# One block's MLP and the next block's differential attention joined in one stage, with the context norm taken into gate and up

## The reference

```python
def first_block(x, ln1, w_in, ..., w_o, ln2, w_gu, w_down, ln_f):
        ...
        x = x + jnp.einsum('btd,de->bte', mix, w_o[l])
        h = rmsnorm(x, ln2[l])
        gate, up = jnp.split(jnp.einsum('btd,df->btf', h, w_gu[l]), 2, axis=-1)
        x = x + jnp.einsum('btf,fd->btd', jax.nn.silu(gate) * up, w_down[l])
    return rmsnorm(x, ln_f)

# second block, differential attention over the latent rows (1024) and the context rows (256)
m = jax.nn.silu(cond) @ w + b                       # ada_modulation: shift, scale, gate
h = rms_norm(x) * norm_gain * (1 + scale) + shift   # once for x, once for ctx
q, k, v, z = jnp.split(h @ w_in, 4, axis=-1)        # then the axial rope on q and k
p = softmax(q k^T); a = p[:, :, 0] - lam * p[:, :, 1]; o = a @ v
y = (rms(o) * subln_gain * (1 - lambda_init) * silu(z)) @ w_out
out = rms_norm(x + gate * y) * final_gain
```

## Time and profile before

| what | value |
|---|---|
| median of three runs | 2417.34 us (2416.16 to 2422.44) |
| the profiled execution's own time | 2417.6 us |
| its span, first to last instruction | 2415.8 us |
| PE busy | 2190.3 us (91%) |
| PE weight load busy | 1780.9 us (74%) |
| DVE busy | 1250.0 us (52%) |
| ACT busy | 988.1 us (41%) |
| POOL busy | 606.5 us (25%) |
| mean granted PE clock | 0.961 |

### The profile page before, as it was taken

How to read it: one execution, slowest core, us unless ns; L and a number is a source line. 1 busy time by engine, 2 the same in 40 slices (tenths; PEclk the granted TensorE clock), 3 DMA queues, 4 the chain that set the end, 5 groups by cost and what they waited for, 6 DMA issues and landing times. The chain is left out here.

```text
span 2415.8 us, 28872 instructions
## 1 busy us (share of the span) xinstructions
PE 2190.3 (91%) x10360; PEld 1780.9 (74%) x10360; DVE 1250.0 (52%) x1667; ACT 988.1 (41%) x1540; POOL 606.5 (25%) x379
## 2 busy tenths in 40 slices
PE   6998989879989999999999937999999999998768
PEld 5886777757768888888888825778777787787557
DVE  4644544445322222223345373767777777777553
ACT  4434444444311111111234242565656656666531
POOL 2212222254012122222444302222223122231140
PEclk9998999989989999999999968999999999999989
DMA  3110000004222212222324212011110111100052
GB/s 111 47 35 19 26 9 26 18 35 136 100 70 69 77 62 78 69 78 97 112 96 158 78 52 70 18 40 40 35 48 22 39 39 35 48 29 28 5 196 104
DMA packets 44526, 148.14 MB, mean 61 GB/s; under 512 B 5025, under 2 KB 5441, under 8 KB 44338
## 3 DMA queue, kind: packets, MB, share of 16 engines
q1 hardware_dynamic: 40610, 133.49, 16.0%
q0 software_dynamic: 3856, 13.86, 1.7%
HBM read 130.28 MB, written 16.78 MB: 61 GB/s over the span
## 5 line engine op out<-in xcount | busy, mean ns | idle before, releaser
L213 PE MATMUL psum<-h_hi,w_hi 128*128 128x512 f32 x704 | 275.3, 391 | 11.8 <-POOL w_lo L198 11.8
L214 PE MATMUL psum<-h_lo,w_hi 128*128 128x512 f32 x704 | 275.0, 391 | 0.0
L215 PE MATMUL psum<-h_hi,w_lo 128*128 128x512 f32 x704 | 274.8, 390 | 0.0
L2215 ACT ACTIVATE diff_probs<-psum,diff_neg_max 128x1280 f32<-128x1280 f32 x128 | 170.2, 1330 | 130.1 <-DVE diff_neg_max L2349 129.1
L2349 DVE TENSOR_REDUCE diff_neg_max<-psum 128x1 f32<-128x1280 f32 x128 | 189.5, 1487 | 55.8 <-PE psum L1918 55.5
L1975 PE MATMUL psum<-h_hi,w_hi 128*128 128x512 f32 x512 | 204.9, 400 | 4.3 <-ACT diff_rstd L2202 2.6
L1673 DVE SCALAR_TENSOR_TENSOR gu_ada_product<-gu_ada_w,gu_cond 128x1024 f32<-128x1024 f32 x48 | 92.6, 1929 | 212.8 <-DMA gu_ada_w<-in_ada_w 209.7
L1976 PE MATMUL psum<-h_lo,w_hi 128*128 128x512 f32 x512 | 201.9, 394 | 0.0
L1977 PE MATMUL psum<-h_hi,w_lo 128*128 128x512 f32 x512 | 201.3, 393 | 0.0
L198 POOL TENSOR_TENSOR w_lo<-w_whole,w_hi 128x1024 fp32r<-128x1024 f32 x44 | 105.2, 2394 | 378.7 <-ACT w_hi L189 378.7
L213 PEld LDWEIGHTS psum<-h_hi,w_hi 128*128 128x128 f32 x704 | 132.8, 189 | 39.8 <-issue 12.2
(11 more groups left out here) (349 smaller groups left out, 4878.5 us busy)
## 6 DMA issues: line engine op xcount, KB each, us to landing
w_whole<-in_w_gu SPq DMA_DIRECT2D x44, 512.0 KB, 3.2
down_w_raw<-in_w_down SPq DMA_DIRECT2D x44, 512.0 KB, 3.2
w_whole<-in_da_w_in SPq DMA_DIRECT2D x32, 512.0 KB, 3.4
gu_ada_w<-in_ada_w SPq DMA_DIRECT2D x24, 512.0 KB, 4.3
w_whole<-in_w_in SPq DMA_DIRECT2D x23, 512.0 KB, 3.4
diff_rope_half<-in_rope SPq DMA_DIRECT2D x17, 512.0 KB, 4.1
mix<-in_x SPq DMA_DIRECT2D x8, 512.0 KB, 8.5
wo_w_raw<-in_w_o SPq DMA_DIRECT2D x8, 512.0 KB, 3.2
```

The source lines that it names most:

```text
L213: pe.matmul(out, wh, rh, start=(k == 0), stop=False)
L214: pe.matmul(out, wh, rl, start=False, stop=False)
L215: last = pe.matmul(out, wl, rh, start=False, stop=(k == KT - 1))
L2215: act.activation(dst, core.psum[:, 1536 * z:1536 * z + NKEY], ACT.Exp, bias=nm[:, qb % 2, z:z + 1], accum_out=rs[:, qb % 2, z:z + 1]).then ...
```

## The change

- In the w_o part PE turns a row tile in two halves (four transposes, two steps of the product, four transposes).
- At the start of gate and up, SP loads the second pair of weight tiles before the modulation's tiles; down's first weights are loaded at the end of gate and up.
- The context norm is done inside gate and up. After tile 14 DVE completes the modulation and scales the context rows, after tile 15 PE turns them into four PSUM banks that gate and up does not use, ACT and DVE split them; SP stores the four parts in DRAM and loads them again before the attention. The gate vector is stored straight from its columns in SBUF, in place of a row made by PE.
- In down, the first half's norms are spread over eight rounds instead of four. The first norm's factor isn't applied before the second's sums: the squares of x and of x times ln_f give both factors at once; POOL scales x3.
- The last round of down ends row tile by row tile. The second half's norms, the turning of both halves and the first head's projections are one list: q of the first half is multiplied feature tile by feature tile while it is turned, then v and k of the first half, then the second half's turn, the context's pieces and q, v and k of the second half. There is no stage boundary between.
- The semaphores are cleared once more, ahead of `block_output`. Buffers of the attention lie where down's buffers were; the loop over the heads is as before.

```diff
@@ Transposes and the w_o tiles
+def pe(self, pe, g, ks=range(KT)):
+    if 0 in ks:
+        pe.wait_ge(self.ready, g + 1)
+    for k in ks:
...
+for t in range(3, NT):
+    op.pe_tile(pe, t, range(0, 4))
+    tr.pe(pe, t - 1, first)
+    op.pe_tile(pe, t, range(4, 6))
+    tr.pe(pe, t - 1, second)
+    op.pe_tile(pe, t, range(6, KT))
...
@@ SP, gate and up
-        load_ada(0)
-        sync.wait_ge(s_st[1], 64)
-        sync.wait_ge(tr.ready, NT)
-        for b in range(2):
-            sync.dma_start(raw[:, b, :], d["w_down"][b, :, :]).then_inc(loaded[b], 16)
-        for i in range(1, EXTRA):
-            load_ada(i)
-        sync.wait_ge(ws.piece_done, first_done(1))
-        load_weights(1)
-        load_ada(EXTRA)
+load_ada(0)
+sync.wait_ge(s_st[1], 64)
+sync.wait_ge(tr.ready, NT)
+sync.wait_ge(ws.piece_done, first_done(1))
+load_weights(1)
+for i in range(1, EXTRA + 1):
+    load_ada(i)
...
+def store_gate(_):
+    sync.wait_ge(s_gate, 1)
+    sync.dma_start(d["gate_row"].rearrange("(k p) -> p k", p=P), core.mods[:, 16:24, 0],
+                   allow_slow_non_contiguous=True).then_inc(s_gate_st, 16)
...
@@ ACT, after its tile 14 of gate and up
+act.wait_ge(s_cx, 16)
+for t in range(2):
+    act.activation(sq[:, :], ctx[:, t, :], ACT.Square, accum_out=ssc[:, t:t + 1]).then_inc(s_css, 1)
+    act.wait_ge(s_css, t + 1)
+act.wait_ge(s_cms, 1)
+act.activation(ssc[:, :], ssc[:, :], ACT.Sqrt).then_inc(s_crt, 1)
+tile(CTX_AT)
+act.wait_ge(s_mods, 1)
+for k in range(KT):
+    act.wait_ge(s_ct, k // 2 + 1)
+    act.activation(hc_made[0][:, k, :], ctx_bank(k), ACT.Identity, scale=core.mods[:, 8 + k, 1:2],
+                   bias=core.mods[:, k, 1:2]).then_inc(s_chi, 1)
+with act.Fori(CTX_AT + 1, FT - 1) as i:
...
@@ DVE, at the same place
+dve.wait_ge(s_ada_done, 2 * 2 * KT + 2)
+for j in range(2):
+    last = dve.tensor_tensor(core.mods[:, 0:16, j], core.mods[:, 0:16, j], core.cols[:, C_ADA:C_ADA + 16], ALU.add)
+step(last)
+for j in range(2):
+    last = dve.scalar_tensor_tensor(core.mods[:, 8:16, j], core.mods[:, 8:16, j], 1.0,
+                                    core.cols[:, C_NG:C_NG + KT], ALU.add, ALU.mult)
+last.then_inc(s_mods, 1)
+dve.wait_ge(s_css, 2)
+dve.tensor_scalar(ssc[:, :], ssc[:, :], 1.0 / D, EPS, ALU.mult, ALU.add).then_inc(s_cms, 1)
+dve.wait_ge(s_crt, 1)
+dve.reciprocal(ssc[:, :], ssc[:, :]).then_inc(s_crec, 1)
+dve.wait_ge(s_crec, 1)
+for t in range(2):
+    last = dve.tensor_scalar(ctx[:, t, :], ctx[:, t, :], ssc[:, t:t + 1], None, ALU.mult)
+last.then_inc(s_cy, 1)
+tile(CTX_AT)
+dve.wait_ge(s_mods, 1)
+for k in range(KT):
...
@@ PE, after its tile 15
+pe.wait_ge(s_cy, 1)
+for k in range(KT):
+    for t in range(2):
+        last = pe.transpose(ctx_bank(k)[:, t * P:(t + 1) * P], ctx[:, t, k * P:(k + 1) * P], core.ident[:, :])
+    if k % 2:
+        last.then_inc(s_ct, 1)
...
@@ PE, last round of down, second half of the tokens
+if g and last:
+    for t in range(4):
+        if t == 3:
+            pe.wait_ge(s_add, 6)
+            for k in range(4):
+                turn.pe(pe, 0, k)
+        for b in range(2):
+            if t == 0:
+                pe.wait_ge(wlo, 2 * FT + b + 1)
+                pe.wait_ge(alo, 2 * FT + b - 1)
+            done = products(g, t, b, False, True)
+        done.then_inc(s_sum, 1)
+    return
+for b in range(2):
...
@@ differential_attention, the first projections
+rows = lead.turn
+pe.wait_ge(lead.s_add, 7)
+ws.wait_tile(pe, 0, "q")
+for k in range(4):
+    rows.pe(pe, 0, 4 + k)
+    first("q0", (k,), split=True)
+first("q0", range(4, KT), split=True)
+ws.wait_tile(pe, 0, "v")
+first("v0")
+pe.wait_ge(lead.s_add, 8)
+pe.wait_ge(s_first_lo, 1)
+first("k0")
+for k in range(4):
+    rows.pe(pe, 1, k)
+pe.wait_ge(lead.s_hc, 32)
+first("vc")
+for k in range(4):
+    rows.pe(pe, 1, 4 + k)
+    if k == 0:
+        pe.wait_ge(s["shuffled"], 1)
+        first("kc")
+    if k == 1:
+        pe.wait_ge(s["v_copied"], 1)
+    first("q1", (k - 1,) if k else (), split=True)
+first("q1", range(3, KT), split=True)
+first("v1")
+first("k1")
+pe.wait_ge(s["shuffled"], 2)
+pe.wait_ge(s["qk_done"], 2 * SPLIT.index("kc") + 2)
+for j in range(3):
+    turn_v(0, j)
+heads(pe, scores, values)
+squares(HEADS2 - 1, 1)
...
@@ DVE there
+lead.add(dve, 4)
+lead.add(dve, 5)
+lead.scaled(dve, 4)
+rows.dve(dve, 0, 0)
+rows.dve(dve, 0, 1)
+lead.add(dve, 6)
+lead.scaled(dve, 5)
+rows.dve(dve, 0, 2)
+rows.dve(dve, 0, 3)
+lead.add(dve, 7)
+lead.scaled(dve, 6)
+rows.dve(dve, 0, 4)
+lead.scaled(dve, 7)
+rows.dve(dve, 0, 5)
+rows.dve(dve, 0, 6)
+dve.wait_ge(lead.s_t, NT)
+rows.dve(dve, 0, 7)
+first_terms("q0")
+lead.means(dve, 1)
+lead.inverse(dve, 1)
+lead.normalised(dve, 1)
+rotated(0, 0)
+for k in range(KT):
+    rows.dve(dve, 1, k)
+first_rest("q0")
+first_terms("k0")
+rotated(0, 1)
+first_rest("k0")
+first_rest("kc")
+first_terms("q1")
+rotated(0, 2)
+first_rest("q1")
+first_terms("k1")
+rotated(0, 3)
+first_rest("k1")
+for j in range(3):
+    v_lo(0, j)
+heads(dve, scores, values)
+gated(HEADS2 - 1, 1)
...
@@ ACT there
+ws.round_hi(act, 0, "q")
+sums(4, 0, 1)
+ws.round_hi(act, 0, "v")
+sums(5, 0, 2)
+sums(4, 1, 3)
+rows.act(act, 0, 0)
+rows.act(act, 0, 1)
+act.wait_ge(s_first_loaded, 16)
+act.activation(first_hi[:, :], first_raw[:, :], ACT.Copy).then_inc(s_first_hi, 1)
+act.wait_ge(ws.loaded[1], 16)
+act.sem_inc(ws.loaded[1], 16)
+act.wait_ge(ws.hi[1], 1)
+act.sem_inc(ws.hi[1], 1)
+sums(6, 0, 4)
+sums(5, 1, 5)
+rows.act(act, 0, 2)
+rows.act(act, 0, 3)
+sums(7, 0, 6)
+sums(6, 1, 7)
+for k in range(4, 7):
+    rows.act(act, 0, k)
+sums(7, 1, 8)
+rows.act(act, 0, 7)
+lead.roots(act, 1)
+first_v("v0")
+for k in range(KT):
+    rows.act(act, 1, k)
+first_v("vc")
+for name in ("q0", "k0", "kc"):
+    first_split(name)
+first_v("v1")
+first_split("q1")
+ws.round_hi(act, 0, "z")
+first_split("k1")
+for j in range(3):
+    v_hi(0, j)
...
@@ program
+with Phase(core, "wo") as po, Phase(core, "gu") as pg, Phase(core, "down") as pd, Phase(core, "diff") as ph:
+    lead = second_half(core, po, pg, pd, mix, mix_at, hid, hid_at)
+    differential_attention(core, ph, mix_at, lead)
+core.clear_semaphores()
```

More of the change, by code:

```diff
@@ L11 @@
 import math
+from collections import namedtuple
 from contextlib import ExitStack
@@ new lines, in second_half @@
+    FIRST_ORDER = (0, 2, 1, 3)
+    first_done = lambda p: 4 + FIRST_ORDER.index(p) + 1
+    loaded = [pd.sem(f"w_loaded{b}") for b in range(2)]
+    whi, wlo, ahi, alo, mm = (pd.sem(n) for n in ("w_hi", "w_lo", "act_hi", "act_lo", "mm"))
+    s_x1 = [pd.sem(f"x{t}") for t in range(NT)]
+    s_row, s_add, s_ss2, s_ms2, s_rt2, s_rec, s_mean = (
+        pd.sem(n) for n in ("row", "added", "squares", "means", "roots", "inverse", "mean"))
+    s_t, s_sum = pd.sem("scaled"), pd.sem("summed")
+    s_x3, s_st3 = pd.sem("x3_ready"), pd.sem("x3_stored")
@@ new lines, in second_half, with rounds @@
+    rows = lambda t: y0[:, t, :] if t < 4 else hid[:, t - 4, :]
+    x3_row = lambda t: hid[:, 4 + t, :] if t < 4 else hid[:, t - 4, :]
+    turn = ModulatedTurn(pd, core, y0, core.hh, core.hl, tmp, lambda k: core.mods[:, 8 + k, 0:1],
+                         lambda k: core.mods[:, k, 0:1])
+    gu_done = 4 + 4 * FT
+    tiles = lambda g: range(4 * g, 4 * g + 4)
+    nothing = lambda _: None
+    def rounds(eng, g, body, stages=()):
+        first = len(stages) if g else 1
+        for i in range(first):
+            body(i, i == 0, False)
+            if g:
+                stages[i](eng)
+        with eng.Fori(first, FT // 2 - 1) as i:
+            body(i, False, False)
+        body(FT // 2 - 1, False, True)
@@ new lines, in weights, with whole, squares @@
+    def weights(g, last, b):
+        return (last_wh[:, b, :], last_wl[:, b, :]) if g and last else (core.wh[:, b, :], core.wl[:, b, :])
+    def whole(pool, g):
+        pool.wait_ge(s_rec, g + 1)
+        if g:
+            pool.wait_ge(turn.ready, 2)
+        for t in tiles(g):
+            pool.tensor_scalar(x3_row(t), rows(t), ss2[:, 0, t:t + 1], 1.0, ALU.mult, ALU.mult).then_inc(s_x3, 1)
+    def squares(act, t, j):
+        act.wait_ge(s_t if j else s_add, t + 1)
+        act.activation(sq[:, :], rows(t), ACT.Square, accum_out=ss2[:, j, t:t + 1]).then_inc(s_ss2, 1)
@@ L2430, in _ @@
-                for z in range(2):
-                    qk_lo(0, 4, z)
                 heads(dve, scores, values)
```

986 lines of the change are left out of this document (522 added, 464 removed).

## The result

| | before | changed |
|---|---|---|
| median | 2416.75 us (4 runs, 2415.33 to 2422.44) | 2390.48 us (4 runs, 2388.29 to 2392.97) |
| span of the profiled execution | 2415.8 us | 2387.9 us |
| PE busy | 2190.3 us | 2177.1 us |
| mean granted PE clock | 0.961 | 0.968 |

The ratio of the changed kernel to the one before is 0.9887, 95% interval 0.9868 to 0.9906: 26.3 us less by the medians, 27.9 by the two spans. The forecast was 2375 in a range of 2357 to 2394: the sign and the range held, and 15 us of the gain were missing. The forecast's own range, 2364 to 2386, did not hold: the measured time is 4.5 us above it, and lies within the stated range only because that was widened for rival C.

A forecast was written before the change was run, and what follows sets the result against it. PE, 91% busy, was taken as the bound, with time to gain or lose only in four places where it waits. Terms -3.6, -13, +20, 0 and -46 sum to -42.6: 2375 us, own range 2364 to 2386, stated 2357 to 2394.

The forecast's parts named there:

- rival C: Last round to first scores: slower handovers or half clock throughout give 98 to 102 us; 2388 us in all, chance 0.18.
- w_o: Among w_o tiles: seven of eight PE waits of 0.52 us for DVE's h_lo go; -3.6 us (0 to -4).
- Start of gate and up: Second tile's weights issued earlier: gap 11.76 becomes 1.3, 2.6 of half clock goes; -13 us (-8 to -13.5).
- Context norm in gate and up: Tiles 15 and 16: PE waits of 6.7 and 8.1 plus 5.2 of half clock; +20 us (+12 to +24).
- At tile 15: Gate and up: ACT waits for DVE's mean behind tile 14's gating, then root, rounding and rest; PE 6.7 us late.
- Tile 16: Gate and up: turns, ACT's eight splits, rounding and POOL's rest; PE's products start 8.1 us after tile 15's end.
- Down: Down's rounds: moved scaling and POOL's x3 covered by PE, which waits for DVE only through the activation's rest; 0 (-2 to +2).
- The tail: Down's last round to first scores: 134.1 us becomes 88 as waiting between stages goes; -46 us (-52 to -36).
- over 85%: Sign in the tail: DVE over 85% busy in the last 25 us before the first score.
- B: Gate and up: no stall at tiles 15 and 16, weights rounded ahead of the context's root; 2358 us, chance 0.12.
- D: Last round to first scores: DVE lengthened by POOL plus sixteen handovers, 118 in place of 88; 2405 us, chance 0.05.
- E: Gate vector's store of 1024 4-byte runs through one or two engines delays down's weights; slower, 2448 or 2526 us, chance 0.03.

The follow-up runs named there:

- run 4: Kernel before with only w_o's turns cut in two halves and the second tile's weights issued ahead of the modulation's loads; 2400.69 us (0.9925).
- run 1: Changed kernel with only DVE's list altered: the context's mean, inverse and scaling moved ahead of the modulation's product; 2374.82 us (0.9807).
- run 2: Changed kernel with only ACT's list altered at tile 16: its first weights rounded ahead of the context's splits; 2381.37 us (0.9847).
- run 3: Changed kernel with both the mean ahead of the modulation's product and tile 16's first weights rounded ahead of the splits; 2363.95 us (0.9771).
- run 6: On top of run 3: ACT's second squares in down one round later, last round starts with the first weight tile for two row tiles; 2354.68 us (0.9742).
- run 7: On top of run 3: in the first half's turn, splits go ahead of the second squares in ACT's and DVE's lists; 2356.46 us (0.9757).
- run 8: On top of run 3: q's first rest, v's turned rests and the rounding of the next head's z weights moved at the chain's end; 2357.81 us (0.9757).
- run 9: Run 3's edits with those of run 6, run 7 and run 8, plus w_o's turn of tile 1 behind tile 2's last products; 2344.81 us (0.9698).
- run 5: Changed kernel with only ACT's list altered: tile 15's first weights rounded ahead of the context's root, DVE's list untouched; 2377.19 us (0.9840).

## Why the prediction was right, and where it was not

*w_o.* Near in number, -4.4 for -3.6, but partly by luck. The sum had only the seven waits of 0.52, and PE's idle time in this stretch did not fall: it is 5.25 us before (107.21 less 101.96 busy) and 5.17 in the change, where 2.24, 0.67 and some waits for weights are new. What fell is the time of the turns themselves. PE's timeline of one turn before, its first four transposes and the product behind it (the other four are the first line of the earlier trace rows, at 576.57):

```profile
575.46 0.60 PE L299 MATMUL psum<-ident,wo_y 128*128 128x128 f32 x4
...
577.43 0.71 PE L1391 MATMUL psum<-wo_w_all_hi,h_hi 128*128 128x512 f32 x2
```

and of half a turn in the change:

```profile
578.17 0.60 PE L301 MATMUL psum<-ident,wo_y 128*128 128x128 f32 x4
578.52 0.71 PE L1393 MATMUL psum<-wo_w_all_hi,h_hi 128*128 128x512 f32 x2
```

From its first transpose to the next product a turn took 1.97 us, and now takes twice 0.35; the second four, which came 0.86 us ahead of the product, are no longer drawn out. That is 1.27 for each of seven turns, 8.9, less the 2.24, the 0.67 and 1.0 more of waits for weights, which leaves 5.0 for the 4.4 measured. The size isn't firm either: with the same code w_o took 102.8 to 103.1 us in four traces and 104.7 or 104.8 in five, so the term is -4.4 or -2.4 by what the clock does behind the 2.24.

*Start of gate and up.* Right in mechanism and size: the gap is 1.45 where 1.3 was forecast, and run 4 shows that the order of issue alone does it.

*Context norm in gate and up.* The step that failed, and the largest miss, is "*At tile 15*: ACT waits for DVE's mean, DVE stands behind the gating of tile 14. From PE's last matmul of tile 14: silu and gating some 1.2". Between the two gatings of that tile stands the modulation's product, and that waits for a transfer which SP issues behind the weights. The step followed ACT's list and DVE's, and not the queue on which DVE itself waits. It measured 14.46 for 6.7: from PE's last matmul of tile 14 (977.06) to DVE's second gating (984.74) it took 7.7 us, where the sum had 0.6, and from there to PE's next product (991.52) the steps took 6.8, for the 6.1 that the sum had left. The steps' lengths were nearly right, and the wait ahead of them was missing. Tile 16 was right (6.62 behind 1.9 of turns, for 6.1 behind 2.0), and the half clock behind both: in the changed kernel's trace the clock was 0.54 and 0.50 in the 4 us behind the two gaps.

```profile
991.50:995.50 4.00, 3.98 (x10) 3.16 (x11) 0.00 (x0) 0.00 (x0) 2.20 (x1) 0.54 0.00 0
1023.60:1027.60 4.00, 3.90 (x9) 3.14 (x10) 3.96 (x6) 0.00 (x0) 3.27 (x1) 0.50 0.00 0
```

It adds up: 14.46 + 6.62 of gaps, 1.9 of turns and some 5 us of half clock, less the 2.6 that no longer fall behind the second tile, give the 25.3 measured. (For the 5 us speak runs 1 and 2, which gained 16.5 and 9.2 us in this stretch, 4.6 more than the two gaps.) Of the 14.7 us by which the spans' difference misses the forecast, this term has 7.9, down 3.0, the tail 2.0 and the two stretches that nothing touched 2.5; the first tile adds 0.2 and w_o takes 0.8 off. Runs 1 to 3 show that none of its gaps was needed.

*Down.* Forecast 0 (-2 to +2), measured +3.0. "Covered by PE, which waits for DVE only through the activation's rest" looked at DVE's load, and the wait was ACT's, for rows that DVE scales in the same round (run 6). The place was not free before either; PE's timeline of the kernel before has

```profile
1290.69 0.70 PE L1809 MATMUL psum<-w_hi,down_a_hi 128*128 128x512 f32 x2 [1.64 <-DVE down_a_lo L1684]
```

so the change raised 1.64 to 3.41, and the 0.83 at 1348.67, for POOL's rest of the weights, is new: together 2.6 of the 3.0. The second was not followed.

*The tail.* 90.1 for 88, and -44 for -46. The chain was forecast as it then ran: k's first product at 44.3, with 43.9 forecast (q's end at 38.5 and a piece of 5.44), the second half's last split at 63.2 (it ends at 1455.52, from 1392.36) with 64 forecast, and behind it DVE's list, 27.0 us for the 24 forecast. Runs 7 and 8 confirm both halves of it. (The pieces behind the 64 add to 24.7, so 88.7 and not 88.) Two things were off. The first two of the four scalings took 1.86 and 2.60 us, beside POOL's rests of weights, and the last two 1.22. And of the last 27 us DVE was busy in 18.7 (16.7 of the last 25, 67% and not over 85%), since it waits there three times 1.45 to 1.47 for POOL's part of the rope, three times 0.69 to 1.33 for ACT's splits and once 0.69 for a load:

```profile
1455.44:1482.45 27.01, 13.56 (x66) 11.16 (x65) 18.67 (x30) 10.43 (x18) 6.13 (x4) 0.83 0.22 78
```

So DVE's list was the bound, and DVE's work was not; that difference is what run 8 used.

*The rivals.* B (no stall in gate and up) is what run 3 built: 2364.0, while B was put at 2358. C and D did not come, although C's margin is what holds the measured time within the range: the tail, of which C speaks, was 2.1 longer than forecast, and the rest of the miss lies elsewhere. That the stated range held is in this sense luck. E did not come either: the store of the gate vector, issued at 1281.29, landed 11.3 us after its issue, within the 12 named, and PE has no gap up to 1303; the one at 1304.07 is down's, which runs 6 and 9 shorten with the store in its place.

*Not shown:* whether the stores' own time moves anything, since that edit was not tried by itself; what the 0.83 in down is; and what makes the 1.0 and 1.5 us in untouched stretches, which lie within the differences between runs.

## What to carry to other kernels

When work is put into another engine's idle time, follow each of its waits to the end, through the queue of the transfer on which the other engine waits: an instruction of 0.16 us on ready data kept PE standing for 14.46 us because it stood behind a load, which stood behind a load. Put what another engine waits for (a rounding of weights) ahead of what waits itself (a root, a split, a square of rows that are still being scaled); two such moves (experiments 1 and 2) were worth 26 us here. A share of 90% busy says nothing of the order of the few places where PE does wait, and the cheapest edit of the whole change, two weight loads ahead of another load, gave some 13 us, the largest gain after the tail's.

## What the runs showed of the hardware

- The load of an activation table took 1.28 us, and where the activation behind it had nothing to wait for, it began 0.02 us later or less, in the trace of before and in all those of the changed kernel's family (986.03 + 1.28, next at 987.33; 970.06 + 1.28, next at 971.36). By the Trainium skill ("ScalarE: Activation LUTs", section "What ACT_TABLE_LOAD costs") a drain of 1380 ns belongs to each switch; in these rows none follows the load.
- The load does not always stand behind its activation's wait: in the changed kernel it ran behind it (986.03), in run 5 ahead of it (970.13, the root at 985.53). There the load cost nothing.
- 1024 runs of 4 bytes took 11.3 us from issue to landing; the 0.152 us per packet of the earlier trace rows, spread over 16 engines, gave 9.7.
- The same gap of PE can leave the clock at full speed or not. Behind the gap of 3.40 us in down the granted clock of the next 4 us was 1.00 in five traces and 0.59 and 0.57 in two (experiments 3 and 5), where the way to the next gap took 46.2 us in place of 44.6. Behind the gap of 2.24 among the w_o tiles it was 1.00 in four traces and 0.65 to 0.68 in five (experiments 2 and 5 to 8), and w_o took 104.7 us or more in place of 103.1 or less.
- DVE's product of two tensors in SBUF (128x1024) took 1.22 us alone and 1.86 and 2.60 beside POOL's subtraction. POOL was at work from 1402.29 for 2.41 us and from 1410.20 for 2.38, DVE from 1403.91 and from 1411.06: both times DVE ended 1.1 us behind POOL's end. The sum of 2.74 us at 1476.14 ended 0.5 behind the end of POOL's subtraction from 1476.00 (2.34 us). So it looks as if DVE stood until POOL was done and did its own work then; no run was made for this.
